# The former expert's combination between the up halves, and final rows made on three engines

## Chip, cores and metric

One core of one Trainium2 chip runs the whole program. The metric is the device time in microseconds of one execution, median of several; the runs of the kernel before gave 1593.97, 1596.10 and 1597.21 us. The span of a profile goes from the first to the last instruction of one execution; the time of that execution is slightly longer.

## The reference

Two transformer-like blocks follow each other on 256 tokens of 1024 numbers, all in float32: a mixer, a mixture of experts (MoE), a second mixer, a second MoE and a final normalisation of each token's row. Only the MoE and the end matter here. In the second block:

```python
    a = jax.nn.silu(tok @ w_gate[e]) * (tok @ w_up[e])
    out = out + combine[:, e:e + 1] * (a @ w_down[e])
...
    x = x + g2 * hier_moe_2(h2, ...)
    return rms_norm(x, final_norm_g)     # x * rsqrt(mean(x*x) + EPS) * g
```

There are 32 experts, each with two matrices of 1024 x 512 (gate, up) and one of 512 x 1024 (down), 2 MB each. A token goes to two of them. The kernel gathers the tokens of an expert into blocks of 32 slots; an expert with more than 32 tokens gets a further block.

## The kernel before, in words

`moe()` runs twice, as first MoE (`last` false) and second MoE (`last` true). A block of 32 slots is one pass of the function `expert(i)`, written once for each engine. On TensorE (PE) a pass is, in order:

- the up product (line L1551): for eight k, four matmuls of gate and up weights against the block `xT`. In the static part the weights are waited for once; in the loop PE waits for the first half of them at k = 0 and for the second half at k = 4 (semaphores `s_half`);
- the gather of the next block (L1510), 16 instructions into bank 5;
- the combination of the former block (L1518, `combine()`), 16 instructions that add `y` times its weights `GwT` into banks 0 to 3, which hold the residual and all experts' sum;
- the down product (L1578), 32 instructions into bank 5. It waits for `s_gT` (the gated block), `s_xg` (DVE has taken the gathered block out of bank 5) and the down weights.

A float32 matmul stands in the trace as two instructions. VectorE (DVE) runs for each block: gate times up (L1794), its transposition (L1798), taking the gathered block (L1668) and making `xT` from it (L1671 or L1673 and L1675), the one-hot matrices of later blocks (L1803, L1806), the weights `GwT` (L1813 to L1815), two counters, and in the second MoE `y` (L1826), which waits for the down product. In the first MoE ScalarE (ACT) writes `y` (L1629). ACT also makes the Silu or sigmoid (L1623). `GwT` is rewritten only after the former combination has read it (`s_comb`).

Thirty blocks are static (`for i in range(STATIC)`). The rest runs in a loop of pairs on every engine, whose count is computed on the chip; with these inputs it is one pair, blocks 30 and 31, in each MoE. SyncE (SP) issues the loads in one queue, by an order written by hand. In the loop, `load_last` (L1434) loads the gate and up weights of a block as four transfers of 1 MB, first halves ahead, after the up product two blocks before, and the down weights (L164) after the down product two blocks before. After the loop PE makes the last combination. In the first MoE PE then runs fillers (`keep_busy`, L181: matmuls of the identity into an unused bank), SP has loaded the weights of mixer 2 (L175) after the last up product, and mixer 2 follows.

The second MoE ends with the final normalisation. ACT squares three of a tile's four groups of 256 columns with a running sum (L1649), DVE the fourth (L1851, L1852). DVE adds and scales, GpSimd (POOL) takes the power -0.5 (L1475). Then DVE makes the two tiles (`tt` = 0, 1) of 128 rows by 1024 columns out of banks 0 to 3 (L1860): sum times root times gain row. SP stores each tile after its row instruction (L1453), and waits for both stores.

Of the kernel before, what the change touches and what calls it, by code (L numbers as in the profile page):

```python
# [5 lines left out]
ALU = mybir.AluOpType  # L6
ACT = mybir.ActivationFunctionType
# [5 lines left out]
P = 128  # L13
D = 1024
# [1269 lines left out]
def moe(c, t, w, last):  # L1284

    nc, ps, h = c.nc, c.ps, c.h
    with phase(nc, w["tag"]) as (st, sb, sem):
# [89 lines left out]
        s_vo = sem("vector_order")  # L1377
        s_sum, s_end = sem("end_squares"), sem("end_rows")
        s_out = sem("out_done")
        VO = 5 if x is None else 6  # L1380

        W = [t[w[x]] for x in ("w1", "w3", "w2")]
# [9 lines left out]
        @block.sync  # L1392
        def _(sp):
            def load_down(i):
                e = bass.ds(i, 1)
                sp.dma_start(downs[down_at(i)].rearrange("p (o n) -> p o n", o=1),
                             W[2][0, e].rearrange("o (p k) f -> p o (k f)", k=KF)).then_inc(s_w2[down_at(i)], 16)

            def load_expert(i):
                u, e, done = i % SETS, bass.ds(i, 1), i - SETS + 1  # L1400
                if done == 1:
                    for half in range(2):
                        sp.wait_ge((s_uph, s_up)[half], 1)
                        cs = slice(half * KD * FF // 2, (half + 1) * KD * FF // 2)
                        for which in range(2):
                            sp.dma_start(c.ring[:, which, cs].rearrange("p (o n) -> p o n", o=1),
                                         W[which][0, e].rearrange("o (p k) f -> p o (k f)", k=KD)[:, :, cs]).then_inc((s_first, sems)[half][which], 16)
                else:
                    sp.wait_ge(s_up, done)
                    load_one(c, sp, sems, u, 0, W, e, third)  # L1410
                    load_one(c, sp, sems, u, 1, W, e, third)
                later = next_down(i - SETS)
                if later is not None:
                    sp.wait_ge(s_down, done)
                    load_down(later)

            for i in range(2, 2 + LEAD + (SETS - 2)):
                load_down(i)
            if mod is not None:
                for m in range(4):  # L1420
                    at = 5 * D + m * 256
                    sp.dma_start(gate_m[32 * m:32 * m + 32, :], row_view(mod, at, at + 256, 32)).then_inc(s_gm, 16)
            sp.dma_start(frow[:], t[w["fg"]].rearrange("(o d) -> o d", o=1).to_broadcast([P, D])).then_inc(s_frow, 16)
            for i in range(SETS, STATIC):
                load_expert(i)
                if x is not None:
                    x.sp_step(sp, i)

            def load_last(u, e, done):
                sp.wait_ge(s_up, done)  # L1430
                for half in range(2):
                    cs = slice(half * KD * FF // 2, (half + 1) * KD * FF // 2)
                    for which in range(2):
                        sp.dma_start(c.ring[:, 3 * u + which, cs].rearrange("p (o n) -> p o n", o=1),  # L1434
                                     W[which][0, e].rearrange("o (p k) f -> p o (k f)", k=KD)[:, :, cs]).then_inc((sems[3 * u + which], s_half[2 * u + which])[half], 16)
                sp.wait_ge(s_down, done)
                load_one(c, sp, sems, u, 2, W, e)

            pairs = count(sp)
            er = sp.alloc_register(w["tag"] + "expert")  # L1440

            def expert_of(i):
                sp.load(er, eid_i[0:1, bass.ds(i, 1)])
                return bass.ds(sp.snap(er), 1)

            with sp.Fori(0, pairs) as q:
                for u in range(2):
                    load_last(u, expert_of(2 * q + (STATIC + u)), 2 * q + (STATIC + u - 1))
            if last:
                o = t["out"].rearrange("b (t p) d -> p (b t) d", p=P)  # L1450
                for tt in range(TT):
                    sp.wait_ge(s_end, tt + 1)
                    sp.dma_start(o[:, tt, :], n[:, tt, :]).then_inc(s_out, 16)  # L1453
                sp.wait_ge(s_out, 16 * TT)
            else:
                sp.wait_ge(s_up, 2 * pairs + STATIC)
                for p in (0, 1, 3):
                    m2_load(c, sp, t, p)
                sp.wait_ge(s_down, 2 * pairs + STATIC)
                m2_load(c, sp, t, 2)  # L1460

        @block.gpsimd
        def _(pool):
            link = lambda ins: c.pch(pool, ins)
            pool.iota(ie[:], [[1, NE]], base=0, channel_multiplier=0, allow_small_or_imprecise_dtypes=True).then_inc(s_ie, 1)  # L1465
            link(pool.iota(ibx[:], [[1, MAXBLK - NE]], base=0, channel_multiplier=0, allow_small_or_imprecise_dtypes=True))  # L1466
            link(pool.iota(ip_i[:], [[0, 1]], base=0, channel_multiplier=1))  # L1467
            link(pool.memset(tri[:], 1.0))  # L1468
            pool.affine_select(out=tri[:], in_=tri[:], compare_op=ALU.is_gt, fill=0.0, base=0,  # L1469
                               pattern=[[1, P]], channel_multiplier=-1).then_inc(s_iota, 1)  # L1470
            if x is not None:
                x.pool_start(pool)
            if last:
                pool.wait_ge(s_stat, 1)
                pool.tensor_tensor(stat[:, 1, 0:TT], stat[:, 0, 0:TT], c.neg_half[:, 0:TT], ALU.pow).then_inc(s_rstd, 1)  # L1475
                return
            pool.wait_ge(s_sum, 4)
            link(pool.tensor_tensor(stat[:, 0, 0:TT], part[:, :, 0], part[:, :, 1], ALU.add))
            link(pool.tensor_scalar(c.rowb[:, 0:TT], stat[:, 0, 0:TT], 1.0 / D, EPS, ALU.mult, ALU.add))
            link(pool.tensor_scalar(stat[:, 1, 2:4], c.rowb[:, 0:TT], EPS, None, ALU.mult))  # L1480
            pool.wait_ge(s_out, 2)
            link(pool.tensor_scalar(stat[:, 0, 2:4], stat[:, 0, 2:4], 1.0 / D, None, ALU.mult))
            link(pool.tensor_tensor(stat[:, 1, 2:4], stat[:, 1, 2:4], stat[:, 0, 2:4], ALU.add))
            link(pool.tensor_tensor(c.hsq[:], stat[:, 1, 2:4], c.neg_half[:, 0:TT], ALU.pow))

        @block.tensor
        def _(pe):
# [39 lines left out]
            def expert(i, q, u):  # L1527
# [8 lines left out]
                for k in range(KD):  # L1536
                    if known and k == 0:
                        pe.wait_ge(s_w1[u], 16 * q + 16)
                        pe.wait_ge(s_w3[u], 16 * q + 16)
                        if i == SETS:  # L1540
                            pe.wait_ge(s_first[0], 16)
                            pe.wait_ge(s_first[1], 16)
                    elif not known and k % 4 == 0:
                        if k == 0:
                            pe.wait_ge(s_w1[u], 16 * q + (16 * TURNS + 16))
                            pe.wait_ge(s_w3[u], 16 * q + (16 * TURNS + 16))
                        else:
                            pe.wait_ge(s_half[2 * u], 16 * q + 16)
                            pe.wait_ge(s_half[2 * u + 1], 16 * q + 16)
                    for j in range(4):  # L1550
                        mm = pe.matmul(ps[32 * j:32 * j + 32, 4, 0:256].rearrange("p (w f) -> p w f", w=2),  # L1551
                                       xT[:, k, :], w13[:, :, k, j * P:(j + 1) * P],
                                       start=(k == 0), stop=(k == KD - 1))
                    if known and i == 0 and k == KD // 2 - 1:
                        mm.then_inc(s_uph, 1)
# [8 lines left out]
                pe.wait_ge(s_Gt, i + 2)  # L1564
                pe.wait_ge(s_y, i + 1)
                gather()
                if not first:
                    pe.wait_ge(s_Gw, i + 1)
                    combine()
                    if x is not None and known and not second:  # L1570
                        x.pe_main(pe, i)

                pe.wait_ge(s_gT, i + 1)
# [31 lines left out]
        def _(act):  # L1605
# [41 lines left out]
            if last:  # L1647
                for tt in range(TT):
                    act.activation(nT[:, 4 * tt:4 * tt + 3, :], acc(tt, 0, 3), ACT.Square, accum_out=part[:, tt, 0:1]).then_inc(s_sum, 1)  # L1649
            else:  # L1650
                for x2 in range(2):
                    if x2:
# [9 lines left out]
        def _(dve):  # L1662
# [192 lines left out]
            dve.tensor_scalar(stat[:, 0, 0:TT], stat[:, 0, 0:TT], 1.0 / D, EPS, ALU.mult, ALU.add).then_inc(s_stat, 1)  # L1855
            dve.wait_ge(s_rstd, 1)
            dve.wait_ge(s_frow, 16)
            for tt in range(TT):
                dst = n[:, tt, :]
                dve.scalar_tensor_tensor(by_m(dst), acc(tt, 0, 4), stat[:, 1, tt:tt + 1], by_m(frow[:]), ALU.mult, ALU.mult).then_inc(s_end, 1)  # L1860


def m2_load(c, sp, t, p):
# [1084 lines left out]
```

## Time and profile before

| | us |
|---|---|
| median of three runs | 1596.1 (1593.97 to 1597.21) |
| the profiled execution | 1594.55 |
| its span | 1592.8 |
| PE busy in the span | 1361.8 (85%) |
| DVE busy | 692.4 (43%) |
| ACT busy | 245.8 (15%) |
| mean granted TensorE clock, of full speed | 0.934 |

A row of the timeline gives the start, the length, the engine, the line, the operation, its output and inputs, and the number of instructions merged into it; in brackets stands how long the engine stood idle before it and what released it. "SPq" and "ACTq" are the sequencers of SP and ACT, which issue DMAs. A row of stretches gives its bounds, its length, the busy time and number of instructions of PE, PEld (weight loads), DVE, ACT and POOL, and then the granted clock (1.00 is 2.4 GHz, 0.50 is 1.2 GHz), the busy share of the 16 DMA engines and what they moved in GB/s. A row of groups gives shapes, count, busy time and the mean of one in ns. Ends of matmuls are modelled, and neighbouring groups overlap a little.

### The profile page before, as it was taken

Reading aid. Unit: us, or ns where it says so; the run is one execution under the profiler, and the core shown is the slowest. Engines: PE = TensorE matmul, PEld = TensorE weight load, DVE = VectorE, ACT = ScalarE, POOL = GpSimd, SP = SyncE. Lnnn points to the kernel's source line nnn. Section 1 sums busy time; section 2 is a strip of 40 time slices with the busy share of each in tenths; the row PEclk is TensorE's granted clock in tenths of the full one; section 3 lists DMA queues with packets and bytes.
Section 4 is the critical chain, followed back from the end, with each engine's and each line's share of the span. In section 5 each row is a group of like instructions: output and inputs, shape, how many; then the busy total and the mean of one; then the engine's idle time right before and its main releaser. Section 6 shows DMA issues by size and latency. Waiting matters only on the chain. (4 is left out here: it accounts for less than half of the span.)

```text
span 1592.8 us, 27696 instructions
## 1 busy us (share of the span) xinstructions
PE 1361.8 (85%) x11926; PEld 879.8 (55%) x11926; DVE 692.4 (43%) x1844; ACT 245.8 (15%) x501; POOL 78.6 (5%) x122
## 2 busy tenths in 40 slices
PE   9999988988978789899999999999886666666665
PEld 8655554544455556588667748886543333333333
DVE  4634654322223343427687536652563233233224
ACT  2322230110001111132222113230200000000000
POOL 2401000000000000030000100100000000000000
PEclk9999999999989999999999999999998888788788
DMA  9955799999999999977531444474999999999996
GB/s 335 275 218 199 307 408 428 417 426 427 425 429 426 425 427 425 378 245 280 188 112 67 135 156 159 164 282 203 369 428 428 430 428 427 429 428 429 430 425 257
DMA packets 94177, 528.55 MB, mean 332 GB/s; under 512 B 8292, under 2 KB 10620, under 8 KB 67944
## 3 DMA queue, kind: packets, MB, share of 16 engines
q1 hardware_dynamic: 89080, 522.35, 81.0%
q0 software_dynamic: 2480, 4.28, 1.3%
q8 instruction: 95, 1.56, 0.4%
q10 hardware_dynamic: 2496, 0.15, 0.1%
q14 instruction: 26, 0.21, 0.0%
HBM read 525.69 MB, written 1.06 MB: 331 GB/s over the span
## 5 line engine op out<-in xcount | busy, mean ns | idle before, releaser
L1551 PE MATMUL ps<-weight_ring,e_xT 128*32 128x256 f32 x3456 | 244.0, 444 | 131.2 <-DMA weight_ring<-in_w_up_dram 87.7
L1551 PEld LDWEIGHTS ps<-weight_ring,e_xT 128*32 128x32 f32 x3456 | 136.2, 127 | 234.1 <-issue 187.4
L1794 DVE TENSOR_TENSOR e_g<-e_act_g,ps 128x128 f32<-128x128 f32 x64 | 24.8, 387 | 269.9 <-ACT e_act_g L1623 268.8
L1792 DVE TENSOR_TENSOR e_act_g<-e_act_g,ps 128x128 f32<-128x128 f32 x32 | 9.2, 287 | 237.6 <-ACT e_act_g L1623 237.5
L1623 ACT ACTIVATE e_act_g<-ps 128x128 f32<-128x128 f32 x64 | 17.8, 278 | 585.1 <-PE ps L1551 585.1
L1551 PE MATMUL ps<-expert_set,e_xT 128*32 128x256 f32 x640 | 56.8, 532 | 53.1 <-DMA expert_set<-in_w_up_dram 53.1
L1578 PE MATMUL ps<-weight_ring,e_gT 128*32 128x256 f32 x1536 | 92.9, 382 | 2.3 <-DMA weight_ring<-in_expert_w_dram 1.0
L2316 PE MATMUL ps<-expert_set,weight_ring 128*128 128x256 f32 x384 | 84.2, 379 | 0.0
L2316 PEld LDWEIGHTS ps<-expert_set,weight_ring 128*128 128x128 f32 x384 | 73.0, 190 | 9.9
L1518 PE MATMUL ps<-e_y,e_GwT 32*128 32x256 f32 x1024 | 76.0, 412 | 1.9 <-DVE e_y L1826 1.3
L1510 PE MATMUL ps<-e_n,e_Gt 128*32 128x256 f32 x1056 | 72.9, 393 | 1.5 <-DVE e_Gt L1717 1.1
L1551 PEld LDWEIGHTS ps<-expert_set,e_xT 128*32 128x32 f32 x640 | 29.5, 152 | 80.2 <-issue 76.2
L1578 PEld LDWEIGHTS ps<-weight_ring,e_gT 128*32 128x32 f32 x1536 | 46.1, 110 | 46.1 <-issue 20.0
L1518 PEld LDWEIGHTS ps<-e_y,e_GwT 32*128 32x128 f32 x1024 | 47.9, 191 | 31.7 <-issue 28.2
L1118 PE MATMUL ps<-ctx_early,e_nT 128*128 128x512 f32 x128 | 59.8, 616 | 4.0 <-DVE e_ctx_kw L1237 4.0
L1126 PE MATMUL ps<-e_nT,ctx_early 128*128 128x256 f32 x256 | 57.4, 382 | 0.0
L2176 PE MATMUL ps<-weight_ring,expert_set 128*128 128x512 f32 x128 | 56.3, 592 | 0.0
L2272 PE MATMUL ps<-weight_ring,expert_set 128*128 128x512 f32 x128 | 55.8, 594 | 0.0
L2163 PE MATMUL ps<-expert_set,weight_ring 128*128 128x256 f32 x256 | 55.4, 379 | 0.0
L1126 PEld LDWEIGHTS ps<-e_nT,ctx_early 128*128 128x128 f32 x256 | 48.0, 190 | 8.9 <-issue 2.7
L2163 PEld LDWEIGHTS ps<-expert_set,weight_ring 128*128 128x128 f32 x256 | 48.6, 190 | 6.6
L1510 PEld LDWEIGHTS ps<-e_n,e_Gt 128*32 128x32 f32 x1056 | 34.9, 112 | 24.7 <-issue 6.3
(592 smaller groups left out, 1933.7 us busy)
## 6 DMA issues: line engine op xcount, KB each, us to landing
weight_ring<-in_expert_w_dram SPq DMA_DIRECT2D x88, 2048.0 KB, 21.1
weight_ring<-in_w_in_dram SPq DMA_DIRECT2D x26, 2048.0 KB, 9.5
weight_ring<-in_w_gate_dram SPq DMA_DIRECT2D x19, 2048.0 KB, 33.7
weight_ring<-in_w_up_dram SPq DMA_DIRECT2D x19, 2048.0 KB, 38.3
weight_ring<-in_w_down_dram SPq DMA_DIRECT2D x18, 2048.0 KB, 39.1
weight_ring<-in_w_ada_dram SPq DMA_DIRECT2D x12, 2048.0 KB, 12.2
expert_set<-in_w_gate_dram SPq DMA_DIRECT2D x10, 2048.0 KB, 32.9
expert_set<-in_w_up_dram SPq DMA_DIRECT2D x10, 2048.0 KB, 37.3
```

Of the source, the lines that this page charges most:

```text
L1118: mm = pe.matmul(ps[:, b, :], nT[:, k8, (b - 6) * P:(b - 5) * P], w[:, k, :], start=(k8 == 0), stop=(k8 == KD - 1), skip_group_check=True)
L1126: mm = pe.matmul(ps[:, b, j * T:(j + 1) * T], w[:, k, at:at + P], nT[:, k8, :], start=(k8 == 0 and j == 0), stop=(k8 == KD - 1), skip_grou ...
L1510: mm = pe.matmul(ps[32 * j:32 * j + 32, 5, 0:256], Gt[:, tt, :], n[:, tt, j * 256:(j + 1) * 256], start=(tt == 0), stop=(tt == TT - 1))
L1518: mm = pe.matmul(ps[:, m, tt * 256:(tt + 1) * 256], GwT[r, tt * P:(tt + 1) * P], y[r, :], start=False, stop=False, skip_group_check=True)
L1551: mm = pe.matmul(ps[32 * j:32 * j + 32, 4, 0:256].rearrange("p (w f) -> p w f", w=2), xT[:, k, :], w13[:, :, k, j * P:(j + 1) * P], start= ...
L1578: mm = pe.matmul(ps[32 * m:32 * m + 32, 5, 0:256], gT[:, j, :], w2[:, j, m * 256:(m + 1) * 256], start=(j == 0), stop=(j == KF - 1))
L1623: act.activation(act_g[:], ps[:, 4, 0:P], gated).then_inc(s_silu, 1)
L1794: dve.tensor_tensor(g[:], spread(act_g[:]), spread(ps[:, 4, P:2 * P]), ALU.mult).then_inc(s_g, 1)
L2163: mm = pe.matmul(ps[:, 4 + j % 4, 0:T], w[:, k, (j % 4) * P:(j % 4 + 1) * P], nT[:, k, :], start=(k == 0), stop=(k == KD - 1))
L2176: mm = pe.matmul(ps[:, 6 + j % 2, :], nT[:, k, tile * P:(tile + 1) * P], w[:, k, :], start=(k == 0), stop=(k == KD - 1))
L2272: mm = pe.matmul(ps[:, j % 4, :], nTp[:, k, tile * P:(tile + 1) * P], w[:, k, :], start=(k == 0), stop=(k == KD - 1))
L2316: mm = pe.matmul(ps[:, 2 + f % 2, 0:T], w[:, k, j * P:(j + 1) * P], rhs[:, k, :], start=(k == 0), stop=(k == KD - 1))
```

## The change

In the loop, the combination of the former block moves from behind the gather to the point between the up halves, ahead of the wait for the second half; five calls of fillers follow it. The static blocks keep their order. At the end, DVE makes three half rows (512 columns), ACT scales the first half of tile 1 into a buffer and POOL multiplies it by the gain row. Tile 0 is one store, tile 1 two, of which ACT issues one.

```diff
@@ pe, expert(): up product, loop part, k = 4
+                            pe.wait_ge(s_y, i + 1)
+                            pe.wait_ge(s_Gw, i + 1)
+                            combine()
+                            keep_busy(c, pe, 7, 5)
                             pe.wait_ge(s_half[2 * u], 16 * q + 16)
                             pe.wait_ge(s_half[2 * u + 1], 16 * q + 16)
...
                 gather()
-                if not first:
+                if known and not first:
                     pe.wait_ge(s_Gw, i + 1)
                     combine()
@@ sp, the stores
-                for tt in range(TT):
-                    sp.wait_ge(s_end, tt + 1)
-                    sp.dma_start(o[:, tt, :], n[:, tt, :]).then_inc(s_out, 16)
-                sp.wait_ge(s_out, 16 * TT)
+                sp.wait_ge(s_end, 1)
+                sp.dma_start(o[:, 0, :], n[:, 0, :]).then_inc(s_out, 16)
+                sp.wait_ge(s_end, 2)
+                sp.dma_start(o[:, 1, 512:D], n[:, 1, 512:D]).then_inc(s_out, 16)
+                sp.wait_ge(s_out, 16 * 3)
@@ pool, after the root
+                pool.wait_ge(s_frow, 16)
+                pool.wait_ge(s_scaled, 1)
+                pool.tensor_tensor(n[:, 1, 0:512], sq[:, 0:512], frow[:, 0:512], ALU.mult).then_inc(s_row0, 1)
@@ act, after the squares
+                act.wait_ge(s_rstd, 1)
+                act.activation(sq[:, 0:512].rearrange("p (m n) -> p m n", m=2), acc(1, 0, 2), ACT.Copy, scale=stat[:, 1, 1:2]).then_inc(s_scaled, 1)
+                act.wait_ge(s_row0, 1)
+                act.dma_start(t["out"].rearrange("b (t p) d -> p (b t) d", p=P)[:, 1, 0:512], n[:, 1, 0:512]).then_inc(s_out, 16)
@@ dve, the rows
-            for tt in range(TT):
-                dst = n[:, tt, :]
-                dve.scalar_tensor_tensor(by_m(dst), acc(tt, 0, 4), stat[:, 1, tt:tt + 1], by_m(frow[:]), ALU.mult, ALU.mult).then_inc(s_end, 1)
+            def row_half(tt, m):
+                return dve.scalar_tensor_tensor(by_m(n[:, tt, :])[:, m:m + 2], acc(tt, m, m + 2), stat[:, 1, tt:tt + 1], by_m(frow[:])[:, m:m + 2], ALU.mult, ALU.mult)
+
+            row_half(0, 2)
+            dve.wait_ge(s_scaled, 1)
+            row_half(0, 0).then_inc(s_end, 1)
+            row_half(1, 2).then_inc(s_end, 1)
```

## Rows read from the trace of the kernel before

**Rows 1.** Waits from 1475 to 1593: who waited for whom, total, times, longest.

```profile
PE ps L1551 <- DMA weight_ring<-in_w_up_dram: 21.5, 5, 5.9
```

**Rows 2.** Stretches: one block of the second MoE.

```profile
1534.00:1548.80 14.80, 8.93 (x128) 4.94 (x129) 4.56 (x15) 0.28 (x1) 0.00 (x0) 0.85 1.00 422
```

**Rows 3.** Timeline of blocks 30 and 31 of the second MoE.

```profile
1562.25 1.05 PE L1510 MATMUL ps<-e_n,e_Gt 128*32 128x256 f32 x16
1562.50 0.28 ACT L1623 ACTIVATE e_act_g<-ps 128x128 f32<-128x128 f32 x1 [6.98 <-PE ps L1551]
...
1567.32 0.43 DVE L1826 TENSOR_TENSOR e_y<-ps,e_gate_m 128x256 f32<-128x256 f32 x1
1568.72 1.93 PE L1551 MATMUL ps<-weight_ring,e_xT 128*32 128x256 f32 x32 [2.49 <-DMA weight_ring<-in_w_up_dram]
1573.67 2.59 PE L1551 MATMUL ps<-weight_ring,e_xT 128*32 128x256 f32 x32 [3.01 <-DMA weight_ring<-in_w_up_dram]
1575.96 2.00 PE L1510 MATMUL ps<-e_n,e_Gt 128*32 128x256 f32 x16
...
1577.89 1.28 PE L1518 MATMUL ps<-e_y,e_GwT 32*128 32x256 f32 x16
1578.00 0.45 DVE L1668 STREAM_TRANSPOSE e_xg<-ps 128x256 f32<-128x256 f32 x1 [0.67 <-PE ps L1510]
...
1579.10 1.93 PE L1578 MATMUL ps<-weight_ring,e_gT 128*32 128x256 f32 x32
...
1581.80 0.42 DVE L1826 TENSOR_TENSOR e_y<-ps,e_gate_m 128x256 f32<-128x256 f32 x1
1582.37 1.15 PE L1518 MATMUL ps<-e_y,e_GwT 32*128 32x256 f32 x16 [1.34 <-DVE e_y L1826]
```

**Rows 4.** Stretches in block 31 of the second MoE: the granted clock.

```profile
1574.50:1575.50 1.00, 1.00 (x19) 0.62 (x12) 0.00 (x0) 0.00 (x0) 0.00 (x0) 0.65 0.54 229
...
1578.00:1578.50 0.50, 0.50 (x8) 0.48 (x12) 0.46 (x2) 0.00 (x0) 0.00 (x0) 0.79 0.00 0
```

**Rows 5.** Load of block 31's down weights, from the line L164.

```profile
L164 SPq DMA_DIRECT2D weight_ring<-in_w_down_dram x1: 333/333/333, 1559.0 to 1559.0; - x1
...
DMA to landing us min/median/max: 19.4/19.4/19.4
```

**Rows 6.** Timeline of block 31 of the first MoE and what follows.

```profile
656.76 3.52 PE L1551 MATMUL ps<-weight_ring,e_xT 128*32 128x256 f32 x32 [2.44 <-DMA weight_ring<-in_expert_w_dram]
661.67 1.93 PE L1551 MATMUL ps<-weight_ring,e_xT 128*32 128x256 f32 x32 [1.39 <-DMA weight_ring<-in_expert_w_dram]
...
666.57 1.93 PE L1578 MATMUL ps<-weight_ring,e_gT 128*32 128x256 f32 x32 [1.02 <-DMA weight_ring<-in_expert_w_dram]
...
669.08 1.15 PE L1518 MATMUL ps<-e_y,e_GwT 32*128 32x256 f32 x16 [0.58 <-ACT e_y L1629]
670.16 6.07 PE L181 MATMUL ps<-ident 128*128 128x128 f32 x52
```

**Rows 7.** Timeline of the end: the final rows and their stores.

```profile
1586.48 2.48 DVE L1860 SCALAR_TENSOR_TENSOR e_n<-ps,e_stat,e_final_row 128x1024 f32<-128x1024 f32 x2 [0.81 <-POOL e_stat L1475]
1587.79 1.53 SPq L1453 DMA_DIRECT2D out_dram<-e_n  x2
```

**Rows 8.** Stretches of the stores' data, the first and the last.

```profile
1588.50:1589.00 0.50, 0.00 (x0) 0.00 (x0) 0.45 (x1) 0.00 (x0) 0.00 (x0) 0.50 0.77 319
...
1591.00:1591.50 0.50, 0.00 (x0) 0.00 (x0) 0.00 (x0) 0.00 (x0) 0.00 (x0) 0.50 0.20 74
```

**Rows 9.** Groups by shape: the nearest instructions of 512 columns.

```profile
L2816 DVE SCALAR_TENSOR_TENSOR weight_ring<-ps,weight_ring 128x512 f32<-128x512 f32 x8 | 5.5, 692 | 0.4 <-PE ps L2298 0.2
L1182 ACT ACTIVATE e_ctx_Vm<-ps 128x512 f32<-128x512 f32 x4 | 2.4, 600 | 16.2 <-PE ps L1118 16.2
L2129 POOL TENSOR_TENSOR expert_set<-expert_set,expert_gain 128x512 f32<-128x512 f32 x1 | 1.0, 1042 | 0.1
```

**Rows 10.** Stretch in which weights of mixer 2 load, in pieces of 2 KB.

```profile
668.00:671.00 3.00, 2.42 (x35) 1.63 (x27) 0.95 (x5) 1.10 (x4) 0.00 (x0) 1.00 1.04 397
```

More of the change, by code:

```diff
@@ L1379, in moe @@
         s_out = sem("out_done")
+        s_scaled, s_row0 = sem("half_scaled"), sem("half_row_ready")
         VO = 5 if x is None else 6
@@ L1566, in expert @@
                 gather()
-                if not first:
+                if known and not first:
                     pe.wait_ge(s_Gw, i + 1)
                     combine()
-                    if x is not None and known and not second:
+                    if x is not None and not second:
                         x.pe_main(pe, i)
```

## The prediction

> **What bounds the kernel now.** I read the waits of the last 120 us first, then the stretches, then the timeline of the last experts, because the change touches nothing before the loops. PE's long waits there are for the gate and up weights [rows 1], and in a stretch of that stage the DMA engines are fully busy at 422 GB/s [rows 2]. The static experts are therefore bound by DMA, and nothing in the change issues a load earlier or makes it smaller. Time can only come from what is left once the last weights are in: the end of the last expert of each MoE, and the final normalisation with its stores.
>
> The last expert of the second MoE is in [rows 3]. Its first half runs at 1568.72 (32 matmuls, 1.93 us). PE waits 3.01 us for the second half and starts it at 1573.67. That half takes 2.59 us, the gather behind it 2.00, where the expert before has 1.05, the combination 1.28, then come the down product (1579.10), y on DVE (1581.80) and the last combination (1582.37). Why the same work is slow: the granted clock falls inside the stretch 1574.50 to 1575.50 (mean 0.65; 0.5 is the 1.2 GHz level, 1.0 is 2.4 GHz) and comes back in the stretch that starts at 1578.00 [rows 4]. Ahead of that fall PE had stood idle for 3.0 us between two bursts of 1.9 and 1.1 us.
>
> **The loop, second MoE.** The combination of the expert before (16 instructions, 1.15 us at full clock) and the fillers now stand between the up halves. A run of 52 filler instructions takes 6.07 us, that is 26 calls of two instructions [rows 6]: 0.117 us each, so five calls add 1.17 us. In the last expert they start when the first half is through, about 1570.6. Their waits are over: the y of the expert before was written at 1567.3 [rows 3], and in the new order about 2.3 us later (its own combination and fillers ahead of its second half), 1569.6 to 1570.1, half a microsecond before it is wanted. Combination and fillers end near 1572.9, 0.7 us before the second half lands: they cost nothing here. If that cover were gone (both at half clock, 4.6 us) the second half would start 1.6 us late. For block 30, whose data is already there, the combination only changes its place and the fillers add 1.17 us, covered by the 2.49 us wait ahead of 1568.72. Nothing is queued to load behind it: SP has issued its last weights before.
>
> What is late next. PE now idles 1.3 us and 0.7 us instead of 2.5 and 3.0, so I take the clock as held. The second half then takes 1.93 us and ACT starts its Silu at 1573.67 + 1.93 + 0.05 = 1575.65 (0.04 to 0.05 after the last matmul, as at 1576.30). From Silu to y, DVE's own chain takes 1567.32 - 1562.50 = 4.82 us in the expert before [rows 3], where neither PE step held it up: y at 1580.47. The other branch is the down product. The combination no longer stands ahead of it, but its weights were issued at 1559.0 and took 19.4 us [rows 5]: they land at 1578.4, so it starts at 1578.5 and ends at 1580.45. Both branches meet at 1580.5, against 1581.80: 1.3 us gained. Moving the combination alone, at the slow clock, is worth nothing: DVE takes x at 1578.00, when the slow gather ends, and from there to y is its own chain of 3.80 us. Bounds: 0, if the clock had not fallen in an execution of before (y is then at 1580.5 too), and 2.2 us if it fell as early as the second half's start (1.93 becomes 3.5, as in [rows 6], and the gather 2.0 rather than 1.05, together 1.6 + 0.95, less what DVE's chain hides). I take 1.3, what this execution shows.
>
> **The loop, first MoE.** Its last expert [rows 6] has its first half at 656.76 (at the slow clock, 3.52 us), its second at 661.67, when the data lands. Before 656.76 PE waits 2.44 us; the 1.17 us of fillers in block 30 go into that wait and should keep the clock, so the first half ends near 658.7, combination and fillers near 661.0, still before 661.67. Then the sign turns. The down product waits for its own weights until 666.57. Until now the combination filled part of that time and PE idled 1.02 us; moved away, it leaves about 1.02 + 1.1 = 2.1 us of idle from the gather's end at 664.5. If the clock falls in it, the 32 matmuls of the down product run at up to 3.52 instead of 1.93 us, with nothing beside them: the y on ACT and the last combination (669.08) follow directly, then the barrier and mixer 2. So between 0 and +1.6 us. The rows nearest to it say both: a gap of 2.44 us ahead of 656.76 brought the slow clock, one of 2.49 us ahead of 1568.72 did not. I take +0.6. Without the fall this MoE changes by 0: the load of the down weights sets 666.57 either way, and SP's loads for mixer 2 wait for the same second half.
>
> **The end.** POOL's root is ready for DVE at 1586.48. Now DVE makes two rows of 1024, 1.28 us each, and SP issues the first store at 1587.79, the second within 1.53 us of it [rows 7]. After: DVE's first half row of 512 takes 0.69 (the nearest row, also one PSUM and one SBUF input) [rows 9], to 1587.17; ACT's scaled copy takes 0.60 [rows 9] to 0.7, so DVE's wait for it ends at 1587.2 to 1587.3; the second half row ends at 1587.95, and the store of tile 0 is issued at 1588.0 instead of 1587.79: +0.2. DVE's last half row ends at 1588.65 and its store follows. POOL starts at 1587.3 and takes 1.04 us for 512 columns [rows 9], so ACT issues the third store near 1588.5. Behind DVE's wait for ACT stand both its remaining pieces; behind ACT's wait for POOL only its own store.
>
> Do smaller and earlier stores help? The store's data flows at 319 GB/s from the first half microsecond of 1588.5 on and stops early in the one of 1591.0 [rows 8]: 1.05 MB in 2.5 us is the full rate, without a gap. The end is set by the first issue and the total of bytes, not by the last piece. So the later first issue counts in full, and the earlier second and third do not. The pieces of 512 columns are rows of 2 KB; loads of such rows run at 397 GB/s [rows 10] against 422 [rows 2], for 0.52 MB 0.08 us more. Sum of the end: +0.25 us. Bounds: +0.6, if POOL takes twice its row or ACT's store comes late, and -0.85 below.
>
> The Trainium skill, page "DMA: Bandwidth & Descriptors", section "Anatomy of one DMA", prices one DMA at about 2.0 us plus its bytes over 436 GB/s; taken for each store by itself, halving the last one would save an estimated 0.6 us, and issued 0.3 us earlier, 0.9. The same page, section "Issuing engines are not separate DMA queues", says that the queues share the engines, and [rows 8] agree: no gap to fill. By that second rule the sum stays as above.
>
> **Sum.** -1.3 (second MoE) + 0.6 (first MoE) + 0.25 (end) = -0.45 us. The profiled execution took 1594.55 us, its span 1592.8 with 1.75 around it; it lies 1.55 below the median of 1596.1, within the spread of 3.2. From 1594.55 comes 1594.1, from the median 1595.65; I give the latter.
>
> **Rivals.**
> 1. Slower: the wait for the first MoE's down weights, no longer filled by the combination, drops the clock at its start (+1.6), and in the second MoE the clock would have held anyway (0); with the end, +1.85: 1597.95. It decides where the 2.1 us gap at 664.5 brings the 1.2 GHz level. For it: 656.76 after 2.44 us. Against: 1568.72 after 2.49 us.
> 2. The stores are no longer one stream: the last quarter lands 0.85 us earlier, counted from its own issue and size. With -1.3 and the first MoE at 0: -2.15, 1593.95. For it: less is left to move after the last DVE instruction. Against: [rows 8].
> 3. The change does not do what it says: the clock falls in spite of the fillers, or fell nowhere before, so y stays bound as it was. Only the end counts: +0.25, 1596.35. For it: the bursts stay short between waits. Against: the remaining idle times are 1.3 and 0.7 us.
> 4. The fillers delay the second half by up to 1.6 us in the second MoE, which with the end gives 1597.95. This needs the clock low at 1568.72, where [rows 3] show 1.93 us for 32 matmuls, the fast value.
>
> **Chances.** Forecast 0.45; rival 1 0.2; rival 2 0.12; rival 3 0.2; rival 4 0.03. The forecast's own span is 1594.3 to 1596.9. What can be told from no change here is 0.2%, 3.2 us, and none of the cases reaches it: the extremes are about -3 and +3 us. With an unforeseen effect in either direction: within 0.2% 0.91, faster 0.04, slower 0.05. The range has to hold the rivals and the spread of the medians: 1593.6 to 1598.3.
>
> **What would show it.** In the profile after: last expert of the second MoE with a second half of 1.93 and a gather of 1.05 us, combination and fillers ahead of it, idle before it under 1 us, y about 6.8 us after the second half's start instead of 8.1. In the first MoE, the down product after its wait at 1.93 us (no fall) or near 3.5 (fall). At the end, the store's data without a gap and ending about 0.25 us later, counted from POOL's root. I am wrong if the last store lands earlier than now counted from that root, if the second half is delayed by the fillers, or if the time moves by more than 3 us.

## The result, and the profile after

The changed kernel took 1597.75 us (median of 20 runs, 1595.2 to 1601.45) against 1595.12 of the kernel before (20 runs beside them). The medians differ by 2.6 us; the ratio on record is 1.0014, interval [1.0008, 1.0021], which is 2.2 us slower, and I go by it. The time is inside my range of 1593.6 to 1598.3 and inside the 0.2% that I called no change, but the sign is clear of noise and I had forecast -0.45 us. Measured once more it was 1.0010 [1.0001, 1.0020]. All ratios here leave out four single runs of 1621.61 to 4693.13 us (one each of `end_only`, `first_only`, `loop_only` and `fill_around` below).

The profiled execution of the changed kernel took 1596.92 us, its span 1595.1. Its timeline of the second MoE's block 31 answers to [rows 3] (PE except where ACT or DVE is named):

```profile
1571.99 1.93 PE L1560 MATMUL ps<-weight_ring,e_xT 128*32 128x256 f32 x32
1573.86 1.15 PE L1523 MATMUL ps<-e_y,e_GwT 32*128 32x256 f32 x16
1574.93 1.38 PE L181 MATMUL ps<-ident 128*128 128x128 f32 x10
1576.94 1.93 PE L1560 MATMUL ps<-weight_ring,e_xT 128*32 128x256 f32 x32 [0.62 <-DMA weight_ring<-in_w_up_dram]
1578.66 1.07 PE L1515 MATMUL ps<-e_n,e_Gt 128*32 128x256 f32 x16
1578.93 0.28 ACT L1632 ACTIVATE e_act_g<-ps 128x128 f32<-128x128 f32 x1 [10.43 <-PE ps L1560]
...
1581.80 1.93 PE L1587 MATMUL ps<-weight_ring,e_gT 128*32 128x256 f32 x32 [2.07 <-DMA weight_ring<-in_w_down_dram]
...
1583.87 0.42 DVE L1839 TENSOR_TENSOR e_y<-ps,e_gate_m 128x256 f32<-128x256 f32 x1 [0.24 <-PE ps L1587]
1584.43 1.15 PE L1523 MATMUL ps<-e_y,e_GwT 32*128 32x256 f32 x16 [0.70 <-DVE e_y L1839]
```

The wait before the second half is 0.62 us, the half 1.93, the gather 1.07: the clock held. From the second half's start to y it is 6.93 us, where [rows 3] have 8.13: the 1.2 us are there. But the reader is to see one more thing: PE now waits 2.07 us ahead of the down product, in the place where the combination used to stand. Here the clock lived through it. The stretches of the same kernel around it:

```profile
1576.94:1578.90 1.96, 1.96 (x37) 1.43 (x41) 0.00 (x0) 0.00 (x0) 0.00 (x0) 1.00 0.59 251
1578.90:1581.80 2.90, 0.84 (x16) 0.32 (x9) 2.42 (x9) 0.28 (x1) 0.00 (x0) 1.00 0.28 119
1581.80:1584.00 2.20, 1.93 (x32) 1.10 (x32) 1.85 (x8) 0.00 (x0) 0.00 (x0) 1.00 0.02 7
```

The first MoE, timeline of PE, answers to [rows 6]:

```profile
657.51 1.93 PE L1587 MATMUL ps<-weight_ring,e_gT 128*32 128x256 f32 x32 [1.13 <-DVE e_xg L1681]
659.26 1.92 PE L1560 MATMUL ps<-weight_ring,e_xT 128*32 128x256 f32 x32
...
663.49 1.93 PE L1560 MATMUL ps<-weight_ring,e_xT 128*32 128x256 f32 x32
...
667.35 1.94 PE L1587 MATMUL ps<-weight_ring,e_gT 128*32 128x256 f32 x32 [1.06 <-DVE e_xg L1681]
669.88 1.15 PE L1523 MATMUL ps<-e_y,e_GwT 32*128 32x256 f32 x16 [0.60 <-DVE e_GwT L1828]
```

PE no longer waits for weights at 659.26: block 30 has become that much longer. Its down product now waits 1.13 us for DVE to take x, a time that the combination had covered. Because block 31 is late, its own down product finds its weights landed and PE idles only 1.06 us ahead of it, not the 2.1 us that I had forecast. The clock held here as well. And the end, answering to [rows 7] and [rows 8], first the timeline, then the stretches of the stores' data:

```profile
1588.54 0.69 ACT L1660 ACTIVATE expert_set<-ps,e_stat 128x512 f32<-128x512 f32 x1 [1.21 <-POOL e_stat L1477]
1588.54 2.13 DVE L1872 SCALAR_TENSOR_TENSOR e_n<-ps,e_stat,e_final_row 128x512 f32<-128x512 f32 x3 [0.81 <-POOL e_stat L1477]
1589.37 1.27 POOL L1480 TENSOR_TENSOR e_n<-expert_set,e_final_row 128x512 f32<-128x512 f32 x1 [0.87 <-ACT expert_set L1660]
1590.03 0.35 SPq L1453 DMA_DIRECT2D out_dram<-e_n  x1
1590.67 0.39 ACTq L1662 DMA_DIRECT2D out_dram<-e_n  x1
1590.69 0.34 SPq L1455 DMA_DIRECT2D out_dram<-e_n  x1
```

```profile
1591.00:1591.50 0.50, 0.00 (x0) 0.00 (x0) 0.00 (x0) 0.00 (x0) 0.00 (x0) 0.50 1.02 410
...
1593.00:1593.50 0.50, 0.00 (x0) 0.00 (x0) 0.00 (x0) 0.00 (x0) 0.00 (x0) 0.50 0.96 365
1593.50:1594.00 0.50, 0.00 (x0) 0.00 (x0) 0.00 (x0) 0.00 (x0) 0.00 (x0) 0.50 0.02 4
```

From DVE's first row to the first issue it is 1.49 us instead of 1.31, and 6.56 instead of 6.32 to the end of the span: +0.24.

So this execution shows -1.2 and +0.24, and is still 2.4 us longer. The difference lies where the change touches nothing. Mixer 2 starts 0.82 us later, since block 29 was 1.0 us late already, and from its first matmul to the first expert's Silu of the second MoE it is 475.8 us against 473.4. The first matmuls of mixer 2, before and after:

```profile
678.36 1.97 PE L2145 MATMUL ps<-ident,expert_set 128*128 128x128 f32 x16 [2.13 <-DVE expert_set L2570]
679.18 2.66 PE L2162 MATMUL ps<-ident,expert_set 128*128 128x128 f32 x16 [2.15 <-DVE expert_set L2587]
```

Here the clock fell in them (granted clock 0.50 from 681 to 683), before it did not. Up to the start of the second MoE that has cost 1.29 us. The other 1.08 us arise in the second MoE's first block, where the clock is at 0.50 from 1145 to 1151, before only from 1145 to 1148. Where it falls differs from one execution to the next, so one pair of profiles cannot carry the verdict. I took stage readings from 18 profiles, and means from the timed runs.

### The profile page after: what moved, and what is told of

Same layout as the page of the kernel before. It is cut to its first block and busy times, and to the rows that moved or that the text cites. A ratio compares the mean times of both kernels' runs of the same rounds, so it can differ in the third digit from the quotient of the medians.

```text
span 1595.1 us, 27785 instructions
## 1 busy us (share of the span) xinstructions
PE 1368.9 (86%) x11966; PEld 887.5 (56%) x11966; DVE 691.7 (43%) x1845; ACT 246.4 (15%) x502; POOL 79.9 (5%) x123
## 3 DMA queue, kind: packets, MB, share of 16 engines
HBM read 525.69 MB, written 1.06 MB: 330 GB/s over the span
```

## The experiments

Each kernel is the one before with the edit named; "ratio" is against the kernel before, with its 95% interval, 10 to 12 runs each (`early_store` has one run). "Moved" is the loop part of the change with its five fillers.

**The parts alone.** `loop_only`: moved in both MoE. `end_only`: the new end. `second_only`, `first_only` (and `first_again`, a repeat): moved in one MoE.

```diff
@@ first_only
+                            if not last:
+                                pe.wait_ge(s_y, i + 1)
+                                pe.wait_ge(s_Gw, i + 1)
+                                combine()
+                            if not last:
+                                keep_busy(c, pe, 7, 5)
                             pe.wait_ge(s_half[2 * u], 16 * q + 16)
...
                 gather()
-                if not first:
+                if not first and (known or not (not last)):
```

> The loop change in both MoE, with the old end. In the profile of the whole change the last y of the second MoE came 1.15 us sooner against block 29, the end took 0.24 us longer, and the executions are some 2 us slower in the mean all the same. Theory A (blocks 30 and 31 of the first MoE have become PE-bound: block 31's first half began at 659.26 without a wait for DMA, so each fall of the clock there is paid): +2 us against before. Theory B (the loss is the end, in executions other than the profiled one): -1.2 us. Theory C (it is neither part, but the place of the later work against the clock's falls, or the code's place): anything, and not the sum of the parts.

> The new final rows and stores alone. Theory A: +0.25 us (the stores are one stream at the full rate, which begins 0.2 us later). Theory B: +2 to +3 us. My prediction's second rival: -0.85 us. In the profile: root to end of span 6.3 us before, 6.56 after.

> The loop change in the second MoE only, old end. Theory A and the prediction: -1.2 us, since y is then bound by the down weights' landing (5.0 us after the second half's start) and DVE's chain, and nothing of the first MoE changes. Theory B: -1.2 us as well. Theory C: not told.

> The loop change in the first MoE only, old end. Theory A: +2 to +3 us, the whole loss. Theory B: within 0.5 us of before. In its profile, by theory A: block 31's first half starts without waiting for its weights, its second half too, and the time from block 30's up product to the last combination, 22.3 us before, is longer, by more when the clock falls in it.

> The loop change in the first MoE alone, once more. Theory D (the gap of 2.1 us ahead of the down product): 0.8 to 2 us slower than before in the mean. If the loss were in the second MoE or the end: 0.

Measured: loop_only 1.0005 [0.9996, 1.0014]; end_only 0.9998 [0.9988, 1.0008]; second_only 0.9999 [0.9989, 1.0009]; first_only 1.0009 [1.0000, 1.0018]; first_again 1.0011 [1.0002, 1.0020]. The end is not the loss (theory B falls); the +0.25 us itself is too small for these intervals. The first MoE alone is slower in both measurements, by 1.4 us (at the edge of noise) and 1.8 us. The second alone gained nothing in the mean, though its interval, -1.8 to +1.4 us, does not exclude the expected -1.2. Its profile shows what can take the gain away; timeline of PE in second_only:

```profile
1574.79 1.93 PE L1557 MATMUL ps<-weight_ring,e_xT 128*32 128x256 f32 x32 [0.61 <-DMA weight_ring<-in_w_up_dram]
1576.51 1.07 PE L1510 MATMUL ps<-e_n,e_Gt 128*32 128x256 f32 x16
1579.83 3.02 PE L1584 MATMUL ps<-weight_ring,e_gT 128*32 128x256 f32 x32 [2.25 <-DMA weight_ring<-in_w_down_dram]
1583.53 2.09 PE L1518 MATMUL ps<-e_y,e_GwT 32*128 32x256 f32 x16 [0.69 <-DVE e_y L1832]
```

The down product takes 3.02 and the last combination 2.09 us: the clock fell after the gap of 2.25. In loop_only the same happened in the first MoE (2.96 and 2.09, then the barrier's fillers 7.03 instead of 6.07). This became theory D: the idle time that the moved combination leaves ahead of the down product lets the clock fall. The profiles of first_only and first_again do not show it: block 31 was late in both, PE idled only 1.12 and 1.09 us there, and the down product took 1.93. What theory D says of the first MoE rests on the profiles of loop_only, change_again and loop_no_fill.

**The gap filled, or fillers without the move.** `fill_wait`: the whole change with 8 calls of fillers in the gap; `fill_wait_old_end`: the same with the old end; `first_filled`, `second_filled`: the same in one MoE. `fill_only`: nothing moved, 5 and 10 calls between the halves of blocks 30 and 31. `fill_around`: nothing moved, 7 calls behind block 30's down product, 9 between block 31's halves, and the end with four stores.

```diff
                 gather()
+                if not known and u == 1:
+                    keep_busy(c, pe, 7, 8)
```

> The whole change, with 8 more calls of fillers (1.9 us) between gather and down product of block 31 in both MoE. Theory D: the clock never falls there, down product 1.93 us in both, end of the first MoE 34.3 us after block 29's Silu, squares of the second at +27.2; against before -0.9 us, against the change 1 to 3 us faster. Rival E: the first MoE stays as slow as in the change, since the gap was not its cause.

> The loop change with 8 further calls of fillers between gather and down product of block 31, old end: the same as the kernel that had them with the new end, for its mean. Theory D: no slow down product in either MoE, -0.8 us against before. Theory F: as slow as the loop change alone, +0.8 us.

> The same with 8 calls of fillers between block 31's gather and its down product in the first MoE. Theory D: no slow down product, 0 against before (the first MoE has nothing to gain), 1 to 2 us faster than the part without them. Rival (the later block 30 costs): as slow as without them.

> The loop change in the second MoE alone, with 8 calls of fillers in its gap. Theory D: -1.2 us against before, the gain that my prediction had for this MoE; second MoE 3.84 us from the down product's start to the squares, never 5.5 or more. Rival (the gap is no loss there): as the second MoE alone, 0 in the mean.

> The kernel before with fillers alone between the up halves (5 calls in block 30, 10 in block 31, behind a wait for the former y); the combination stays behind the gather, where it fills the wait for the down weights. Theory D (what the change gives is the held clock of the second half, what it loses is the idle gap of 2.1 us that the moved combination leaves ahead of the down product, in which the clock falls in some executions and slows the down product to about 3 us, the last combination and what follows): second MoE as in the change, squares 27.2 us after block 29's Silu instead of 28.3, no gap over 1.2 us ahead of the down product in either MoE, so never a slow one; -1.2 us against before. Rival E (fillers themselves delay block 31 through block 30, which is PE-bound with them): the first MoE longer by 0.5 us or more from block 29's Silu to its end (34.5 before), total 0 or slower.

> The order of before; 7 calls of fillers behind block 30's down product, 9 between the halves of block 31, no others; the end with four stores. Theory D: no idle over 1.3 us in block 31, block 31's first half at 1.93 us in either MoE, second MoE 27.2 to 27.4 us from block 29's Silu to squares; -1.2 and -0.35 from the end, -1.5 us against before. Theory E (fillers delay): first MoE longer than 34.5 by 0.5 us or more.

Measured: fill_wait 0.9996 [0.9987, 1.0005], fill_wait_old_end 0.9994 [0.9986, 1.0003], first_filled 1.0006 [0.9997, 1.0015], second_filled 0.9985 [0.9975, 0.9995], fill_only 0.9993 [0.9984, 1.0002], fill_around 0.9995 [0.9986, 1.0004]. The pair that differs by the eight fillers alone, with the new end: 1.0014 and 1.0010 without, 0.9996 with; the intervals of 1.0014 and 0.9996 do not touch. With the old end it is 1.0005 without and 0.9994 with, for the second MoE alone 0.9999 and 0.9985, for the first 1.0009 and 1.0011 against 1.0006. All go the same way, but in these three the intervals overlap, so for either MoE by itself the gain from the fillers is not shown from the times. second_filled is the one kernel here that is clear of noise on the fast side by itself, by 2.4 us; its interval (0.8 to 4.0 us) holds the 1.2 expected. In second_filled, PE's timeline:

```profile
1574.21 1.93 PE L1557 MATMUL ps<-weight_ring,e_xT 128*32 128x256 f32 x32 [0.64 <-DMA weight_ring<-in_w_up_dram]
1575.93 1.07 PE L1510 MATMUL ps<-e_n,e_Gt 128*32 128x256 f32 x16
1576.94 2.05 PE L181 MATMUL ps<-ident 128*128 128x128 f32 x16
1579.08 1.93 PE L1586 MATMUL ps<-weight_ring,e_gT 128*32 128x256 f32 x32
```

fill_only was a half miss for D: its first-MoE reading was fine, but in the second MoE the clock fell 0.5 us into block 31's first half, behind an idle time of 2.41 us (the half took 3.24 us). The fillers started late and in part ran slowly, and the second half started 5.92 us after the first instead of 4.95: rival E is real where the clock is already down. The change's own five fillers show the same in the first MoE. In fill_wait, fill_wait_old_end and first_again block 31's first half was slow (3.02 to 3.33 us) and the second half started 5.88 us behind it instead of 4.91. In the first two, which have the eight fillers of the gap as well, the down product came 0.8 us later for it (10.6 us after the first half's start against 9.8 in before and first_again). The fillers in the gap are not free.

**The whole change again, and the move without fillers.** `loop_no_fill` is loop_only without the `keep_busy`.

> The whole change once more, for its mean and for one more execution to read. So far, in ten profiles, the clock fell ahead of or in the down product of block 31 in 2 of the 6 places where the combination had moved and nothing had been put in its place, and in none of the 14 others. Theory D: +1 to +2 us against before; where the profile has a down product of about 3 us, the stretch from its start to the end of that MoE is 5.7 to 5.9 us instead of 3.7 to 3.85, else not. Theory F (the moved combination costs in every execution, by the later block 30): the first MoE is longer without a fall.

> The combination moved in both MoE, no fillers, old end. Theory D: both gaps of block 31 stay open (1.9 us ahead of the second half, 2.1 ahead of the down product), the clock falls in one of them in most executions; +0.5 to +2 us against before. The prediction's view (the order alone is worth nothing, the idle before the second half is what matters): 0. In a profile without a fall: second MoE from block 29's Silu to squares 27.2, with one 28.3 or more.

Measured: 1.0010 [1.0001, 1.0020] and 1.0016 [1.0007, 1.0025]. Moving the combination without fillers, which the prediction held to be worth nothing in the second MoE, is 2.6 us slower over both; its profile has a down product of 3.39 us in the first MoE, and in the second a first half of 2.57 and a moved combination of 2.09. In change_again the clock fell in both gaps. Its timeline of PE, first MoE, then second, and the stretches of the second:

```profile
664.38 1.93 PE L1560 MATMUL ps<-weight_ring,e_xT 128*32 128x256 f32 x32 [0.59 <-DMA weight_ring<-in_expert_w_dram]
666.10 1.07 PE L1515 MATMUL ps<-e_n,e_Gt 128*32 128x256 f32 x16
669.26 3.46 PE L1587 MATMUL ps<-weight_ring,e_gT 128*32 128x256 f32 x32 [2.09 <-DMA weight_ring<-in_expert_w_dram]
673.29 1.15 PE L1523 MATMUL ps<-e_y,e_GwT 32*128 32x256 f32 x16 [0.57 <-ACT e_y L1638]
...
1583.29 2.72 PE L1587 MATMUL ps<-weight_ring,e_gT 128*32 128x256 f32 x32 [2.21 <-DMA weight_ring<-in_w_down_dram]
1586.69 2.09 PE L1523 MATMUL ps<-e_y,e_GwT 32*128 32x256 f32 x16 [0.69 <-DVE e_y L1839]
```

```profile
1580.00:1583.30 3.30, 1.09 (x23) 0.52 (x16) 2.58 (x10) 0.28 (x1) 0.00 (x0) 1.00 0.26 109
1583.30:1584.30 1.00, 1.00 (x20) 0.76 (x24) 0.93 (x4) 0.00 (x0) 0.00 (x0) 0.99 0.00 0
1584.30:1586.00 1.70, 1.70 (x20) 0.55 (x9) 0.63 (x3) 0.00 (x0) 0.00 (x0) 0.50 0.00 0
```

The clock (last but two) is at 2.4 GHz through the gap and goes to 1.2 one microsecond into the down product.

All 18 profiles have two blocks 31 each. The stage is read from the start of the down product to the first square (or the first residual) behind the last combination:

| block 31 | places | slow down product | stage, first MoE | stage, second MoE |
|---|---|---|---|---|
| moved, idle ahead of it 2.07 to 2.25 us | 8 | 5 (2.72 to 3.46 us) | slow 5.2 to 5.7 | 3.84 to 3.94, slow 5.55 and 5.85 |
| moved, not filled, idle only 1.06 to 1.12 us | 3 | 0 | 3.7 | none |
| moved, gap filled | 7 | 0 | 3.73 | 3.84 |
| combination in its old place | 18 | 0 | 3.7 | 3.8 to 4.7 |

The first row holds three places of the first MoE, all slow, and five of the second, two of them slow. The second row is the first MoE of after, first_only and first_again, where block 31 was late. And in the second MoE with the old order and no fillers between the halves, the clock fell in the second half in all 6 profiles (2.58 to 3.43 us); with the change's fillers in none.

**The stores.** `early_store`: the kernel before with the new end, in which DVE's first half row is stored at once, so four stores. `fill_and_early` adds fill_only, `second_filled_early` adds second_filled.

```diff
-            row_half(0, 2)
+            row_half(0, 2).then_inc(s_end, 1)      # and one more store on SP
```

> The kernel before with the new end, in which DVE's first half row is stored at once: four stores of 256 KB. My reading (the stores are one stream at the full rate whose end is its first issue plus all bytes): the first issue comes 0.6 us earlier than before, the end 0.3 to 0.5 us earlier, 6.6 us from POOL's root to the end of the span instead of 7.05 (the change has 7.29). Rival (each store costs its own fixed time and size, the last one decides): as in the change, 7.3.

> Fillers alone in the loops and the end with four stores. Theory D with my reading of the stores: the sum of both, -1.2 - 0.4 = -1.6 us against before. Rival E: 0.

> The loop change in the second MoE alone with its gap filled, and the end with four stores. Theory D with my reading of the stores: -1.2 - 0.35 = -1.5 us against before, from POOL's root to the end of the span 6.7 us, second MoE 3.84 us from the down product to the squares. If the stores' fixed time decided: -1.0 us, and 7.3.

Measured: from POOL's root to the end of the span 6.69, 6.74 and 6.76 us, and 6.75 in fill_around; 7.01 to 7.10 in the ten profiles with the old end, 7.28 to 7.31 in the four with the change's. SP and POOL in early_store:

```profile
1587.41 1.71 SPq L1454 DMA_DIRECT2D out_dram<-e_n  x3
1587.47 1.27 POOL L1479 TENSOR_TENSOR e_n<-expert_set,e_final_row 128x512 f32<-128x512 f32 x1 [0.87 <-ACT expert_set L1655]
```

The first issue comes 1.50 us after the root begins, where before it was 2.04. Of these 0.54 us about 0.3 reach the end. In the times: early_store one run, 1594.36; fill_and_early 0.9994 [0.9985, 1.0003]; second_filled_early 0.9990 [0.9979, 1.0000]. The last is 1.6 us faster than before, at the edge of noise, and not told apart from second_filled. The gain of the earlier store is shown in the profiles and not in the times.

## Why the prediction was wrong

**Second MoE, -1.3: the mechanism was right, the sum was not.** The second half at 1.93, the down weights as the bound, y 1.2 us sooner: all as written (down product at 1581.80, 4.86 us after the second half's start; I had 4.83). The step that failed is "What is late next. PE now idles 1.3 us and 0.7 us instead of 2.5 and 3.0, so I take the clock as held", and rival 3's "the remaining idle times are 1.3 and 0.7 us". They left out a third: a few sentences on, I had the down product wait until 1578.5 with the combination gone, and did not count the 2.1 us in front of it as idle. A fall there costs 1.7 to 2.0 us, more than was won. The clock fell in 2 of the 5 such places of this MoE, and the second MoE alone gave 0.9999, where -1.3 us would be 0.9992; its interval holds both.

**First MoE, +0.6: right mechanism, too small.** I saw the gap of 2.1 us, gave a term between 0 and +1.6, and named its fall as rival 1, the case that came true in sign. That its 1597.95 is close to the measured median is partly luck: it assumed one fall in every execution and a second MoE that gains nothing. The first MoE alone measured +1.4 and +1.8 us. In the profiles 3 of 6 places were slow, all three with an idle time of 2.08 or 2.09 us; in the other three the gap was only about 1.1 us, which I had not foreseen. The price of a fall is 1.5 to 1.95 us to the end of the MoE, since in one of them the last combination was slow too (2.09 instead of 1.15), which the bound of 1.6 had left out, and there 0.8 more in the barrier's fillers.

**Block 30: mis-sized.** I added 1.17 us of fillers; it became 2.3 longer (from block 30's first half to block 31's 9.9 us in the first MoE, against 7.6 without the wait for weights before) because DVE's taking of x, once behind the combination, is now waited for (1.13 us). In 3 of the 9 first MoE with the moved combination block 31's first half starts without a wait for weights, so the slack that I had counted was gone there.

**The end, +0.25: right.** +0.24 in this pair of profiles and 0.2 to 0.3 over all of them, by the reason given (first issue +0.2, one stream at the full rate). Sized wrong inside it: POOL's multiplication took 1.27, not 1.04, and still cost nothing, as ACT's store was queued in time. Rival 2 did not decide. Nor did the fixed cost that the Trainium skill, page "DMA: Bandwidth & Descriptors", section "Anatomy of one DMA", gives for each DMA; it is fitted there to DMAs issued by GpSimd, which the prediction did not say, and these stores are issued by SP and ACT. What the Trainium skill says on the same page, section "Issuing engines are not separate DMA queues", agrees with these rows: with stores of SP and ACT under way together, the stretches show 365 to 410 GB/s and no gap. The four-store end points the same way: first issue 0.54 us earlier, end about 0.3 earlier.

**The sum over executions.** With falls in 5 of the 11 unfilled places, the profiles' terms give +0.8 (first MoE), -0.3 (second: -1.2 and +0.9), +0.25 (end): +0.75 us, an estimate. Measured are +1.6 and +2.2. The rest stays open, and theory C, the place of the later work against the clock's falls, is not excluded for it. From mixer 2's first matmul to the second MoE's first expert Silu it took 471.8 to 475.9 us in the profiles, by where the clock falls at the start of mixer 2 and in the second MoE's first block; in the six whose first MoE has the unfilled gap the mean is 474.0, in the twelve others 473.1. PE idles 2.00 to 2.16 us ahead of mixer 2's first matmuls in all 18, and the clock fell there in 4 of the six and in 3 of the twelve, at 1.3 us each. The change may make these falls more likely; so few profiles do not show it.

## What to carry to other kernels

When work is moved into one wait of PE, list every wait that it leaves behind, with its new length, and price it as open or as filled; fillers cover such a wait at a cost of their own when PE comes to it late. Here the combination moved in the second MoE alone, with fillers in both waits, was faster (0.9985). The other way, real work left in the wait for the down weights and fillers between the halves, gave 0.9993 to 0.9995, which is not told from no change. Where a fall of the clock depends on its place in the execution, one profile shows a mechanism, and only several show its share. Stores that run as one stream at the full rate end sooner by an earlier first issue, not by a smaller last piece.

## What was not expected

An idle of 2.07 to 2.25 us ahead of block 31's down product was followed by a fall of the clock in 5 of 8 cases, one of 1.06 to 1.12 us in none of 3. The fall came up to one microsecond after PE had started again (the rows of change_again above). The clock's cost is therefore paid by the work behind the gap, and is not seen in the gap itself.
